# A two-layer mixer block plus an SSD/conformer block on one core: the first layer's windowed attention regrouped by pairs of heads, its PSUM banks split by stage, its values projected like its keys

## The reference, cut to what matters

```python
q, k, v, gate_a, u, gate_b = split_cols(hn @ w_in, (512, 128, 128, 512, 512, 512))
q = rms_norm(q.reshape(L, 8, 64), q_g); k = rms_norm(k.reshape(L, 2, 64), k_g); v = v.reshape(L, 2, 64)
att = swa_sink_attention(q, k, v, sinks, rel_bias) * silu(gate_a)   # band: own block of 128 and the one before
ssm = s5_mixer(u, ...) * silu(gate_b)       # state space scan, gelu, then a gated linear unit ("GLU")
out = concat([att, ssm]) @ w_out
```

## Time and profile before

| | |
|---|---|
| median of three runs | 2299.91 us |
| profiled execution | 2298.77 us, its span 2297.5 us |
| PE, DVE, ACT, POOL busy in the span | 92%, 61%, 39%, 32% |
| mean granted TensorE clock | 0.953 of full |
| slots, from the bias tile to the last `outputs` | 95.75 to 331.70 us |
| attention | 331.70 to 471.44 us |

### The profile page before, as it was taken

The page is one execution under the profiler, slowest core; times in us unless marked ns, Lnnn a source line. Parts: engine busy times, 40 slices in busy tenths (PEclk is TensorE's granted clock), DMA queues, the critical chain, the costliest instruction groups (busy, mean ns, idle before and its releaser), DMA issues.

```text
span 2297.5 us, 24584 instructions
## 1 busy us (share of the span) xinstructions
PE 2116.1 (92%) x9420; PEld 1617.5 (70%) x9420; DVE 1394.1 (61%) x1998; ACT 900.8 (39%) x1475; POOL 732.6 (32%) x560
## 2 busy tenths in 40 slices
PE   7998888899999999989999899999998898979996
PEld 5778775478865767656668677888776666767785
DVE  6254445631224688935434779899995767762647
ACT  5333238642334576134422334443222233442532
POOL 3465530035310111145536400000004665215744
PEclk9997898899999999999999999999999998989998
DMA  4311231024240111221122211121133213345222
GB/s 155 114 52 31 74 111 69 14 92 174 97 128 15 38 46 58 80 83 46 47 112 86 87 65 65 47 65 55 55 105 104 63 46 138 124 142 215 101 74 101
DMA packets 71342, 193.74 MB, mean 84 GB/s; under 512 B 10990, under 2 KB 20367, under 8 KB 70968
## 3 DMA queue, kind: packets, MB, share of 16 engines
q1 hardware_dynamic: 71224, 192.16, 24.7%
HBM read 148.70 MB, written 46.71 MB: 85 GB/s over the span
## 4 chain that ended last, share of the span: by engine, by line
PE 63%; DVE 12%; ACT 8%; POOL 7%; DMA 5%; issue 4%; SPq 2%; DVEq 0%; ACTq 0%; POOLq 0%
PE psum L262 59%; POOL m L307 4%; PE psum L265 2%; DMA m<-in_w 2%; DVE m L2663 1%; ACT m L297 1%; SPq L1515 1%; DVE m L2741 1%; DMA m<-scr_cgscr 1%; DVE m L402 1%; ACT m L1258 1%; DMA scr_hscr<-m 1%; DVE m L1900 1%; PE psum L1773 1%; DVE m L2748 1%
## 5 line engine op out<-in xcount | busy, mean ns | idle before, releaser
L262 PE MATMUL psum<-m,m 128*128 128x512 f32 (+9 forms) x8520 | 1996.6, 397 | 138.4 <-POOL m L307 33.1
L262 PEld LDWEIGHTS psum<-m,m 128*128 128x128 f32 (+3 forms) x8520 | 1510.9, 193 | 598.7 <-issue 180.8
L307 POOL TENSOR_TENSOR m<-m,m 128x1024 fp32r<-128x1024 f32 (+1 forms) x130 | 327.7, 2524 | 1110.3 <-ACT m L297 1110.3
L2663 DVE SCALAR_TENSOR_TENSOR m<-m,m,m 128x1024 f32<-128x1024 f32 x240 | 308.1, 1285 | 6.3
L297 ACT ACTIVATE m<-m 128x1024 fp32r<-128x1024 f32 (+2 forms) x166 | 173.5, 1049 | 282.6 <-PE psum L262 191.2
L265 PE MATMUL psum<-m,m 128*128 128x128 f32 x840 | 124.3, 287 | 26.8 <-DVE m L857 11.1
L265 PEld LDWEIGHTS psum<-m,m 128*128 128x128 f32 x840 | 102.1, 147 | 51.3 <-issue 16.4
L1900 DVE TENSOR_SCALAR_CACHE_REDUCE m<-m,m 128x896 bf16<-128x896 f32 (+4 forms) x130 | 102.7, 846 | 1.0
L2024 DVE CUSTOM_DVE_ANT_0 m<-psum,m 128x128 f32<-128x128 f32 (+3 forms) x64 | 48.2, 754 | 54.2 <-POOL m L2225 19.6
L2225 POOL TENSOR_TENSOR m<-m,m 128x384 f32<-128x384 f32 (+5 forms) x48 | 72.1, 1524 | 10.6 <-DVE m L2024 10.6
L2130 ACT ACTIVATE m<-m,m 128x1024 bf16<-128x1024 f32 (+1 forms) x62 | 64.1, 1037 | 23.6 <-DVE m L1927 23.6
(11 more groups left out here) (300 smaller groups left out, 1754.3 us busy)
## 6 DMA issues: line engine op xcount, KB each, us to landing
m<-in_w SPq DMA_DIRECT2D x164, 512.0 KB, 3.5
scr_hscr<-m SPq DMA_DIRECT2D x4, 2048.0 KB, 6.6
m<-scr_hscr SPq DMA_DIRECT2D x4, 2048.0 KB, 11.8
scr_turned<-scr_strip SPq DMA_DIRECT2D x8, 575.5 KB, 12.1
m<-in_x SPq DMA_DIRECT2D x8, 512.0 KB, 8.5
scr_gscr<-m SPq DMA_DIRECT2D x16, 256.0 KB, 4.2
m<-in_x SPq DMA_DIRECT2D x2, 2048.0 KB, 9.0
m<-scr_turned SPq DMA_DIRECT2D x8, 512.0 KB, 3.5
```

The source lines that it names most:

```text
L262: return self.nc.tensor.matmul(out, lhsT, rhs, start=start, stop=stop, skip_group_check=True)
L307: k.nc.gpsimd.tensor_tensor(lo, raw, hi.bitcast(F32), ALU.subtract).then_inc(*k.up("w_lo", i))
L2663: V.scalar_tensor_tensor(o, u[:, j:j + 1024], w[:, j:j + 1], o, ALU.mult, ALU.add).then_inc(*up("cv_tap", m, j))
```

## The change

- `E.slots` now has two value slots (wide halves, like `kk`): PE projects v with tokens along the row, ACT copies it to `VT` (the second gate buffer), PE turns it by four `tr` per half into a bank of `E.mis`, ACT copies that to `VN`. The cut at 25 slots stays, so 13 gate halves come before the attention and 3 are late.
- A unit is block b by pair p: tiles 2p and 2p+1 of q, each with a head in partitions 0 to 63 (key head 0) and one in 64 to 127 (key head 1). `s1` goes back and forth between the halves and writes one bank per half; `s3` writes both halves of the partitions of one bank, 256 wide each.
- Banks: logits `E.S` 3 to 6 (two units), turns `E.PB` 7 and 0, output `E.OB` 1, late gates `E.GB` 2, GLU `E.glu` 3 to 6. PE issues s1 one unit ahead.
- A late gate is Tanh of half the argument on ACT, then `(tanh + 1) * x` on DVE, with the factor one half put into the GLU's product (gates of the attention half are all early).
- ACT does the four Gelus in a row in pass 6, the high parts in passes 9 to 12; POOL instead of DVE subtracts their low parts and that of the attention's first half.

```diff
+        self.S = Ring(k, "ev_S", [3, 4, 5, 6], [("free", "ev_mis", *use) for use in (("VR", 7), ("VI", 7), ("K", 7), ("Y", 7))])
+        self.PB = Ring(k, "ev_PB", [7, 0], [("qk_rt", "q"), ("free", "ev_proj", "g", 5, 0)])
+        self.OB = Ring(k, "ev_OB", [1], [("free", "ev_proj", "g", 5, 1)])
+        self.GB = Ring(k, "ev_GB", [2], [("free", "ev_proj", "g", 6, 0)])
+        self.glu = Ring(k, "ev_glu", [3, 4, 5, 6], [("free", "ev_S", 7, p, h) for p in range(2) for h in range(2)])
...
-        self.slots += [("v", j, 0) for j in range(4)] + [("g", m, half) for m in range(8) for half in range(2)]
+        self.slots += [("v", 0, half) for half in range(2)] + [("g", m, half) for m in range(8) for half in range(2)]
         self.slots, self.late = self.slots[:25], self.slots[25:]
-        self.units = [(b, h) for b in range(8) for h in range(2)]
+        self.units = [(b, p) for b in range(8) for p in range(2)]
+        self.four = [(h, i) for h in range(2) for i in range(2)]
...  tensor_even
+    def values(half):
+        bank = k.bank(E.mis.take("VT", half))
+        pe.wait_ge(*E.mis.freed("VT", half))
+        pe.wait_ge(*at("v_t", half))
+        for j in range(4):
+            ins = k.tr(bank[:, 128 * j:128 * j + 128], E.VT[:, 512 * half + 128 * j:512 * half + 128 * j + 128])
+        ins.then_inc(*up("v_ps", half))
...
-            for b in (2 * m, 2 * m + 1):
-                bank = k.bank(E.proj.take("v", b))
-                pe.wait_ge(*E.proj.freed("v", b))
-                pe_rows(k, "vv", b, bank[:, 0:128]).then_inc(*up("v_ps", b, also=[done("vv")] if b == 7 else ()))
...  s1
+        banks = [k.bank(E.S.take(b, p, h)) for h in range(2)]
+        for i in range(2):
+            for h in range(2):
+                hl = slice(64 * h, 64 * h + 64)
+                ins = k.mm(banks[h][:, 256 * i:256 * i + nk], E.QT[hl, 2 * p + i, 128 * b:128 * b + 128], E.KT[hl, k0:k0 + nk], i == 0, True)
...  s3
-            ins = k.mm(bank[hl, :], E.VN[:, k0 // 128 + c, hl], pt[:, c, :], c == 0, c == nk // 128 - 1)
+            for h in range(2):
+                hl = slice(64 * h, 64 * h + 64)
+                ins = k.mm(bank[hl, 0:256], E.VN[:, k0 // 128 + c, hl], pt[:, c, 256 * h:256 * h + 256], c == 0, c == nk // 128 - 1)
...
+    s1(*E.units[0])
     for i in range(n + 3):
-        if i < n:
-            s1(*E.units[i])
+        if i + 1 < n:
+            s1(*E.units[i + 1])
...  vector_even
+    def late_gate(m, half):
+        o = E.gev[m % 2][:, 512 * half:512 * half + 512]
+        dve.wait_ge(*at("g_tanh", m, half))
+        V.scalar_tensor_tensor(o, o, 1.0, k.bank(E.GB[("g", m, half)]), ALU.add, ALU.mult).then_inc(
+            *up("g", m, half, also=[("free", "ev_GB", "g", m, half)]))
...  the loop: s1(i), late_gate of pass i-1, s1b(i-1), s3(i-3)
+        if E.late_gate(i - 1):
+            late_gate(*E.late_gate(i - 1)[1:])
-            V.tensor_tensor(E.YL[:, m, :], E.YF[m], E.YH[:, m, :].bitcast(F32), ALU.subtract).then_inc(*up("y_lo", m))
-        if i == 16:
-            att_low(0)
...  scalar_even
+        if ("g", m, half) in E.late:
+            A.activation(o, bank, ACT.Tanh, scale=0.5).then_inc(*up("g_tanh", m, half))
+        else:
+            A.activation(o, bank, ACT.Silu).then_inc(*up("g", m, half, also=[("free", "ev_proj", "g", m, half)]))
...
-        if 4 <= i <= 7:
-            m = i - 4
+        if i == 6:
+            for m in range(4):
...  pool_even, in the attention's loop
+        if 9 <= i <= 12:
+            m = i - 9
+            pool.wait_ge(*at("y_hi", m))
+            G.tensor_tensor(E.YL[:, m, :], E.YF[m], E.YH[:, m, :].bitcast(F32), ALU.subtract).then_inc(*up("y_lo", m))
+        if i == 15:
+            pool.wait_ge(*at("att_hi", 0))
+            G.tensor_tensor(E.half(E.ML, 0), E.half(E.GA, 0), E.half(E.MH, 0).bitcast(F32), ALU.subtract).then_inc(*up("att_lo", 0))
```

More of the change, by code:

```diff
@@ L747, in tensor_even, with s1 @@
         ssm(s)
-    def s1(b, h):
+    def s1(b, p):
         nk, k0 = E.band(b)
[L751 to L759, removed]
@@ L802, in tensor_even @@
             for what, col in (("gate", 128), ("lin", 0)):
-                bank = k.bank(E.mis.take("glu", what, m, half))
-                pe.wait_ge(*E.mis.freed("glu", what, m, half))
+                bank = k.bank(E.glu.take(what, m, half))
+                pe.wait_ge(*E.glu.freed(what, m, half))
                 for q in range(4):
@@ L1021, in s1 @@
             dve.wait_ge(*last("s5_Y"))
-        for m in range(4):
-            ps = k.bank(E.mis[("S", b, h, m // 2)])[:, 256 * (m % 2):256 * (m % 2) + nk]
-            dve.wait_ge(*at("swa_S", b, h, m // 2))
-            V.scalar_tensor_tensor(Lv[:, m], ps, E.RQ[:, 8 * b + 2 * m + h:8 * b + 2 * m + h + 1], E.BIA[:, 4 * h + m, 256 - nk:256], ALU.mult, ALU.add).then_inc(
-                *up("swa_L", b, h, m, also=[("free", "ev_mis", "S", b, h, m // 2)] if m % 2 else ()))
+        dve.wait_ge(*at("swa_S", b, p))
@@ L1027, in s1 @@
+        for j, (h, i) in enumerate(E.four):
+            ps, col = k.bank(E.S[(b, p, h)])[:, 256 * i:256 * i + nk], 8 * b + 4 * p + 2 * i + h
+            V.scalar_tensor_tensor(Lv[:, j], ps, E.RQ[:, col:col + 1], E.BIA[:, 4 * h + 2 * p + i, 256 - nk:256], ALU.mult, ALU.add).then_inc(
+                *up("swa_L", b, p, j, also=[("free", "ev_S", b, p, h)] if i else ()))
         dve.wait_ge(*last("swa_L"))
-        V.tensor_reduce(nm, Lv, AX.X, ALU.max, negate=True).then_inc(*up("swa_max", b, h, 0))
+        V.tensor_reduce(sb[:, 0:4], Lv, AX.X, ALU.max, negate=True).then_inc(*up("swa_max", b, p, 0))
@@ L1228, in scalar_even @@
         elif kind == "v":
-            for b in (2 * m, 2 * m + 1):
-                if b == 0:
-                    root(*late)
-                act.wait_ge(*at("v_ps", b))
-                if b == 0:
-                    for i in range(2):
-                        act.wait_ge(*at("u_out", i))
-                A.activation(E.VN[:, b, :], k.bank(E.proj[("v", b)])[:, 0:128], ACT.Copy).then_inc(*up("v", b, also=[("free", "ev_proj", "v", b)]))
-            if m == 3:
+            if half == 0:
+                root(*late)
+            act.wait_ge(*at("qk_ps", kind, m, half))
+            A.activation(E.VT[:, 512 * half:512 * half + 512], k.bank(E.proj[(kind, m, half)]), ACT.Copy).then_inc(
+                *up("v_t", half, also=[("free", "ev_proj", kind, m, half)]))
+            if half:
                 act_panel(k, 13)
+                values(0)
         else:
+            if (m, half) == (0, 0):
+                values(1)
             gate(m, half)
@@ L1311, in scalar_even @@
                 k.marks(act, "ev_att", ("pe", "dve"))
[L1312 to L1313 removed]
+            A.activation(sb, k.bank(E.glu[("gate", m, half)]), ACT.Sigmoid, bias=k.sm("glub")[:, 4 + m:5 + m]).then_inc(
+                *up("glu_sig", m, half, also=[("free", "ev_glu", "gate", m, half)]))
             if (half, m) == (0, 0):
```

169 lines of the change are left out of this document (90 added, 79 removed).

## The result

Four runs of the changed kernel gave a median of 2261.54 us (2259.54 to 2265.18), four of the kernel before, beside them, 2298.79 (2297.61 to 2303.29): a ratio of 0.9829, 95% interval 0.9806 to 0.9851. Forecast were 2258 us and a range of 2240 to 2278. The profiled execution took 2261.08 us, its span is 2259.8.

The account below looks back on a forecast made before the run. No engine was taken as full in the attention, units passing from hand to hand; the value round had a bank stop and low clock. Terms -12 - 10 - 24 + 4 = -42 from 2298.77 gave 2257, as median 2258 us; range 2240 to 2278.

Parts of the forecast that it names:

- the third step: Attention from exp of unit 7 to exp of unit 15: 43 us instead of 66.6, a gain of 24.
- steps near 5.2 from unit 9 on: Sign of being right, in the attention: exp of unit to exp of unit takes near 5.2 us from unit 9.
- a POOL operation beside a long small step of DVE: Sign of being wrong, in the attention: POOL's work running while a small DVE step takes long.
- 1, values, -12: Value round before the attention: wide halves instead of narrow slots make it 12 us shorter, bounds -8 and -16.
- step 2: Attention up to exp of unit 7: 10 us earlier, with two gates fewer and fewer table loads.
- step 5: Allowance for PE's clock falling in the attention: +4 us, six units at 5.8 instead of 5.2.
- step 4: Low parts moved from DVE to POOL: cost 0, up to 4 us if POOL holds DVE's small steps.
- (b): Rival: the value round doesn't shrink, its spread tile or bank as late as before: 2270 us; chance 0.09.
- (d): Rival: only the value round gains; the Gelu block and low clock behind it eat the rest: 2287 us; chance 0.07.
- (a): Rival: handing over itself, not the ring, sets the attention's unit; units keep 7 us: 2271 us; chance 0.14.
- (c): Rival: the pairs don't overlap in the attention, units 6.5 us on the whole: 2267 us; chance 0.08.
- (e): Rival: slower, PE at 1.2 GHz for the whole attention and pairs not overlapping: 2327 us; chance 0.04.

Follow-up runs that it names:

- kernel 1: The kernel before with only the two value slots as wide halves, units, ring, Silu and Gelus as before: 2277.95 us, ratio 0.9879.
- kernel 3: The changed kernel with Silu on ACT for the three late gates, without DVE's product: 2262.78 us, ratio 0.9810.
- kernel 9: The changed kernel with the edits of kernel 7 and kernel 8 together: 2253.86 us, ratio 0.9782.
- kernel 7: The changed kernel with the heads' outputs one pass later, on PE ahead of the turns of the next unit: 2258.34 us, ratio 0.9805.
- kernel 8: The changed kernel with ACT's four high parts right behind the Gelus and POOL's low parts beside them, passes 5 to 8: 2257.43 us, ratio 0.9807.
- kernel 2: The changed kernel with units by key head again, so no pairs; banks and look-ahead as changed: 2266.58 us, ratio 0.9829.
- kernel 6: The changed kernel without the four low parts of the Gelu rows, which POOL zeroes early: 2257.98 us, ratio 0.9806.
- kernel 5: The changed kernel with the four low parts of the Gelu rows back on DVE, in passes 10 to 13: 2256.72 us, ratio 0.9805.
- The repeat: The changed kernel, unaltered, run again beside three other kernels on one chip: 2262.36 us, ratio 0.9823.
- kernel 4: The changed kernel with logits, turns and outputs in one ring of banks 3 to 6 and logits not ahead: 2296.58 us, ratio 0.9951.
- kernel 10: The changed kernel with own banks kept, but the logits of a unit issued in its own pass: 2273.03 us, ratio 0.9868.

## Why the prediction was right, and where its terms were off

The forecast was 3.5 us low, and the case that came true is its likeliest; but the third step, more than half of its sum, was right in size by luck. Of its signs, steps near 5.2 from unit 9 on didn't come (4.8 and 7.5 in turn), and one sign of being wrong did, a POOL operation beside a long small step of DVE. By its steps:

*1, values, -12.* `outputs` was forecast near 198 and began at 197.52; the last `outputs` of the mixer stands at 314.67 instead of 327.17, so -12.5. The spread tile, the stop of 1.19 and the clock came as worked out. What the step left out is in step 2: run alone (kernel 1), the edit brings 22.8 us at the GLU, since its two freed slots take two gates out of the attention. The prediction saw the gates and booked them to the attention; the sum doesn't care, a reader who asks which edit pays does. Taken first, the values are more than half of the gain, 22.8 of 40.5 at the load and 1.21 of 1.71% by the ratios. In the working, the bank of L1002 is wanted by the second value slot, not the third, since a slot of narrow values takes two banks; the sum doesn't change.

*2, up to exp of unit 7, -10.* 394.40 to 372.82 is -21.6, less the 12.5 is -9.1. The block came as forecast: two loads, Gelus of 2.0, 10.7 us from load to exp. Kernel 1 alone brings 18.1 of the 21.6; what the other edits add up to here is 3.5, little over the scatter of a landmark, and isn't divided among them. Six of the 14 table loads saved were worth nothing (kernel 3); the other eight were not put back by themselves. In the working, 32 us from 333 is 365, not 361; exp of unit 6 came 1.3 ahead of its 372 all the same (358.20 + 12.5). The Trainium skill, ScalarE: Activation LUTs, section What ACT_TABLE_LOAD costs, gives 2.66 us with a drain; this trace has 1.28, the copy ahead of the load done at 362.13 and the Gelu 0.01 behind it, and the trace decides.

*3, exp 7 to 15, 43 with +4 for the clock (step 5).* 46.5: the two terms together are right to 0.5, and that is luck. The first two units came as worked out, 3.83 and 7.27 against 4.2 and 7.5, with turn and output behind the Gelu block at the lower level and DVE waiting 4.20 for them. The last six took 35.4 against 6 x 5.2 + 4 = 35.2, but of other parts. DVE's 4.9 us a unit was too much: undisturbed it is 4.48 (kernel 9), six of them 26.9. POOL's hold, put at nothing, adds 6.7 (step 4), and unit 15 adds 1.8, with turns of 1.97 and outputs of 1.61 at the lower level again. So the clock's allowance had a reason, but shows in one of the six units. The granted clock fell in others too (0.52 from 400 to 405), beside DVE's held steps.

```profile
375.00:380.00 5.00, 3.68 (x16) 2.34 (x16) 0.95 (x4) 5.00 (x17) 0.00 (x0) 0.50 0.01 3
...
400.00:405.00 5.00, 5.00 (x24) 3.26 (x23) 4.86 (x11) 5.00 (x16) 2.39 (x1) 0.52 0.00 0
...
410.00:415.00 5.00, 2.93 (x14) 2.22 (x16) 3.78 (x11) 4.44 (x17) 0.00 (x0) 0.67 0.00 0
```

What PE's order and its clock cost together is the 4.0 of kernel 7; in kernel 8 the same order adds 0.4 to a step of 4.48 at the upper level and 2.1 at the lower. Of the 20.1 that the stretch fell from 66.6, 5.7 come with kernel 1, in which a late gate has left it. The pairs overlapped as expected, 1.13 for eight logit instructions and 1.08 for eight outputs, these in one bank; they paid some 2.4 to 3.8 us ahead of the GLU (kernel 2), which no ratio shows. The tail to the GLU grew by 1.5 us, 419.31 to about 431.2 (eight outputs of 1.08 from 430.22) against 10.4. PE's last outputs wait 0.53 for the product of the unit before, which frees the only output bank; ahead of them two lots of turns took 1.97 and one of outputs 1.98, where 1.09 and 1.08 stand at the upper level.

*4, low parts on POOL, cost 0, up to 4.* This step failed: the cost put at nothing is 6.7 us of held DVE steps in the stretch. Without the low parts 3.2 to 3.5 come back, since a DVE that is held less waits longer for outputs (kernel 6); where it doesn't wait for outputs, the hold costs the whole 6.7 (kernel 7), over the bound of 4. Back on DVE, the low parts cost no more than on POOL (kernel 5).

*After the GLU.* Forecast was no shift. ACT's Sigmoid is 40.2 us earlier (434.29 against 474.54), the end of the span 37.7. The repeat gave back more, 43.7 at the load and 37.4 at the end. The stretch from the GLU's load to the end runs the same instructions and took 1825 to 1834 us in these kernels, 1825.2 before and 1834.3 with one ring, which is slow ahead of it. Nearly all of these 9 us stand in the first 300 behind the load: 1335 TensorE instructions stand there in before and 1293 in kernels 4 and 9, 42 fewer at some 0.22 us each. The granted clock from 200 to 250 us and from 250 to 300 us behind the load is 0.98 and 1.00 in before, 0.88 and 0.93 in these two. What lowers it there is left open, and kernel 10, as long but at 0.91 and 1.00, must lose part of them elsewhere. With these 9 us about, a landmark ahead of the GLU says more of an edit here than one run's total.

The rivals: (b) and (d) fall with the value round and the loads. (a), that handing over itself and not the ring sets the unit, is wrong: with own banks a unit takes 46.5 / 8 = 5.8 us, with one ring and no look-ahead 9.0 (kernel 4), with own banks and no look-ahead 6.2 (kernel 10). (c) was priced at 9 us; kernel 2 has no overlap, and the same ratio. (e) needed PE as the bound; PE is busy 30.72 of 46.49 us. The range's own lower end is 2246 by the three terms that the prediction gives for it, 4 us each below 2258, and not 2242; the measured time is far from both.

## What to carry to other kernels

When work moves to an engine that is idle, look in the profile at what it will run beside: here four subtractions of 1.22 us left VectorE for GpSimd, and from there held VectorE's small steps for 6.7, so that the move gained nothing. In a loop handed from engine to engine, first break the ring of waits (own banks, one unit ahead); only then does it matter how long each engine works. Ask of each edit what else it moves: the smallest edit here, two slots instead of four, gave more than half.

## What the runs showed of the hardware that was not expected

A scaling of 128x256 and a join of 128x4 on VectorE, both out of and into SBUF, ended within 0.2 us of the end of a GpSimd subtraction of 2.35 to 2.39 us that ran beside them, though two of the first need 0.62 and one of the second 0.16; a reduction begun before isn't lengthened (1.22). Outputs into two halves of the partitions of one bank overlap: eight instructions in 1.08 us, where eight logit instructions of the same width out of one half took 1.99 before. TensorE rested 11.4 us in the Gelu block and took 1.97 for the eight turns behind it, at a granted clock of 0.50, and 1.09 for the next eight.
